# The last feed-forward chunk by token halves, and the last layer norm from row sums

## The reference

```python
def layer_norm(x, g, b):
    mu = mean(x); var = mean((x - mu)**2)
    return (x - mu) * rsqrt(var + 1e-5) * g + b
def swiglu(x, w_gate, w_up, w_down):
    return (silu(x @ w_gate) * (x @ w_up)) @ w_down
x = layer_norm(alpha*x + 0.5*swiglu(x, ffn1...), ln1)
x = layer_norm(alpha*x + hybrid_mixer(x), ln2)
x = layer_norm(alpha*x + memory_cross_attention(x, mem), ln3)
x = layer_norm(alpha*x + 0.5*swiglu(x, ffn2...), ln4)
```

## Time and profile before

| | us |
|---|---|
| median of 3 runs | 1303.44 |
| lowest and highest | 1303.38, 1303.83 |
| profiled execution, its own time | 1306.2 |
| its span, first to last instruction | 1304.4 |
| TensorE busy (matmuls) | 1268.3, 97% |
| VectorE busy | 715.5, 55% |
| ScalarE busy | 449.2, 34% |
| GpSimd busy | 90.4, 7% |
| mean granted TensorE clock | 0.992 |

### The profile page before, as it was taken

The page is one execution under the profiler, slowest core; times in us unless marked ns, Lnnn a source line. Parts: engine busy times, 40 slices in busy tenths (PEclk is TensorE's granted clock), DMA queues, the critical chain, the costliest instruction groups (busy, mean ns, idle before and its releaser), DMA issues.

```text
span 1304.4 us, 16284 instructions
## 1 busy us (share of the span) xinstructions
PE 1268.3 (97%) x6065; PEld 1050.1 (81%) x6065; DVE 715.5 (55%) x994; ACT 449.2 (34%) x699; POOL 90.4 (7%) x126
## 2 busy tenths in 40 slices
PE   7999999999998999999999999999999999999995
PEld 6888888888887887877778887888888888888884
DVE  4644444444475666565644557554664444444446
ACT  3322222222245654455533325342422222222221
POOL 2000000000032100001010030002300000000004
PEclk9999999999999999999999999999999999999998
DMA  7433333333327222222163205213343333333311
GB/s 228 144 96 96 96 96 96 96 96 96 96 66 211 81 82 71 59 56 59 49 209 98 96 33 177 82 49 97 97 129 96 96 96 96 96 96 96 96 48 65
DMA packets 163129, 128.03 MB, mean 98 GB/s; under 512 B 5120, under 2 KB 150544, under 8 KB 163088
## 3 DMA queue, kind: packets, MB, share of 16 engines
q1 hardware_dynamic: 159872, 116.44, 29.8%
q0 software_dynamic: 3008, 11.01, 2.4%
q10 hardware_dynamic: 208, 0.01, 0.0%
HBM read 123.25 MB, written 4.19 MB: 98 GB/s over the span
## 4 chain that ended last, share of the span: by engine, by line
PE 91%; DVE 3%; POOL 2%; DMA 1%; ACT 1%; issue 1%; SPq 0%; DVEq 0%; POOLq 0%; ACTq 0%
PE bank L601 19%; PE bank L603 19%; PE bank L602 19%; PE banks_scores L601 9%; PE banks_scores L603 9%; PE banks_scores L602 9%; PE bank L880 2%; PE bank L862 1%; DVE ring_lo L1406 1%; PE banks_scores L832 1%; PE banks_scores L831 1%; DVE stats L1438 1%; PE bank L619 1%; DMA raw<-in_ffn_w_gate 1%; DVE xT_lo L1406 1%
## 5 line engine op out<-in xcount | busy, mean ns | idle before, releaser
L1406 DVE TENSOR_TENSOR ring_lo<-raw,ring_hi 128x1024 fp32r<-128x1024 f32 x215 | 261.0, 1234 | 123.6 <-ACT ring_hi L1090 123.3
L601 PE MATMUL bank<-xT_hi,ring_hi 128*128 128x512 f32 (+1 forms) x728 | 280.6, 385 | 4.5 <-DVE ring_lo L1406 2.3
L1090 ACT ACTIVATE ring_hi<-raw 128x1024 fp32r<-128x1024 f32 x215 | 221.7, 1056 | 176.5 <-DMA raw<-in_ffn_w_up 89.4
L602 PE MATMUL bank<-xT_lo,ring_hi 128*128 128x512 f32 (+1 forms) x728 | 278.4, 382 | 0.0
L603 PE MATMUL bank<-xT_hi,ring_lo 128*128 128x512 f32 (+1 forms) x728 | 278.3, 382 | 0.0
L601 PEld LDWEIGHTS bank<-xT_hi,ring_hi 128*128 128x128 f32 x728 | 138.8, 191 | 31.0 <-issue 3.9
L603 PEld LDWEIGHTS bank<-xT_hi,ring_lo 128*128 128x128 f32 x728 | 138.7, 191 | 26.3
L602 PEld LDWEIGHTS bank<-xT_lo,ring_hi 128*128 128x128 f32 x728 | 138.9, 191 | 24.9
L601 PE MATMUL banks_scores<-xT_hi,ring_hi 128*128 128x512 f32 (+1 forms) x368 | 140.7, 382 | 0.0
L602 PE MATMUL banks_scores<-xT_lo,ring_hi 128*128 128x512 f32 (+1 forms) x368 | 140.3, 381 | 0.0
L603 PE MATMUL banks_scores<-xT_hi,ring_lo 128*128 128x512 f32 (+1 forms) x368 | 140.3, 381 | 0.0
(11 more groups left out here) (274 smaller groups left out, 1783.0 us busy)
## 6 DMA issues: line engine op xcount, KB each, us to landing
raw<-in_ffn_w_gate SPq DMA_DIRECT2D x44, 512.0 KB, 4.7
raw<-in_ffn_w_up SPq DMA_DIRECT2D x44, 512.0 KB, 4.4
raw<-in_ffn_w_down SPq DMA_DIRECT2D x44, 512.0 KB, 3.3
raw<-in_mix_w_in SPq DMA_DIRECT2D x34, 512.0 KB, 3.8
raw<-in_mem_w_k SPq DMA_DIRECT2D x8, 512.0 KB, 4.1
raw<-in_mix_w_out SPq DMA_DIRECT2D x8, 512.0 KB, 3.2
raw<-in_mem_w_v SPq DMA_DIRECT2D x8, 512.0 KB, 3.2
raw<-in_mem_w_q SPq DMA_DIRECT2D x8, 512.0 KB, 4.7
```

What stands on the lines that cost most here:

```text
L601: pe.matmul(dst, hi, mhi, start=start, stop=False)
L602: pe.matmul(dst, hi, mlo, start=False, stop=False)
L1090: nc.scalar.activation(dst, src, copy).then_inc(unit_hi, 1)
L1406: nc.vector.tensor_tensor(dst, src, hi.bitcast(F32), ALU.subtract).then_inc(done, 1)
```

## The change

In the second feed-forward layer the loop runs nine times. What is left (gate and up of chunks 20 and 21, the down pairs 9 and 10) is written out in a function `closing` on TensorE, ScalarE and VectorE. TensorE's order there is: gate and up of chunk 20; gate and up of chunk 21 for the first 256 tokens; pair 9 and then pair 10 for the tiles of blocks 0 and 1; gate and up of chunk 21 for the other 256 tokens; pair 9 for tiles 4 to 6, pair 10 for 4 and 5, pair 9 for tile 7, pair 10 for 6 and 7. Pairs 9 and 10 of a tile are accumulated in one PSUM bank, and VectorE adds a tile once for both. The hidden values of the pair 10 have buffers of their own (`end_hi`, `end_lo`), and those of chunk 21 are made in two token halves.

Blocks 0 and 1 are normed as before, with the gain on VectorE and the bias on GpSimd. For blocks 2 and 3 the two tile additions also give row sums; VectorE makes minus the mean of them and centres the block with the gains in one operation into `x_mid`; ScalarE squares the block less its mean with a running sum, and scales that and adds eps; GpSimd takes the power -0.5; VectorE finishes each block in two halves, and each half is stored by itself. A constant `eps` is filled at the start.

```diff
+                def closing(n, chunk, pair):          # TensorE
+                    def up_half(p):
+                        for m in range(2):
+                            ready(n + 4 + m)
+                            half_units(n + 4, 1, p, (m,), end_up)
+                    def down_part(j, units, hid, first, last):
+                        for m in range(2):
+                            mm = down_product(units, j, m, hid, first, last)
+                        return mm
+                    gate_up(0, n, chunk)
+                    pe.wait_ge(h_full, chunk)
+                    up_half(0)
+                    ready(n + 3)
+                    pe.wait_ge(h_lo_done, chunk)
+                    for p in range(2):
+                        for j in range(4 * p, 4 * p + 4):
+                            if p == 0:
+                                pe.wait_ge(sums, tile_sums(f, pair - 1, j + 5))
+                            else:
+                                pe.wait_ge(end_sums, j - 3)
+                            if j == 7:
+                                pe.wait_ge(end_lo_done, 3)
+                                for early in (4, 5):
+                                    down_part(early, n + 6, (end_hi, end_lo), False, True).then_inc(end_tiles, 1)
+                            down_part(j, n + 2, (h_hi, h_lo), True, False)
+                        ready(n + 7)
+                        pe.wait_ge(end_lo_done, 2 + p)
+                        for j in range(4) if p == 0 else (6, 7):
+                            down_part(j, n + 6, (end_hi, end_lo), False, True).then_inc(end_tiles, 1)
+                        if p == 0:
+                            up_half(1)
...
-                with pe.Fori(0, FF_PAIRS - 1) as i:
+                with pe.Fori(0, FF_PAIRS - 1 - f) as i:
...
+                def closing(n, chunk):                # ScalarE
...
+                    prep(n + 6)
+                    prep(n + 7)
+                    act.wait_ge(end_h, 1)
+                    high(end_hi[:, 0, :], hf[:, 0, :], end_hi_done)
+                    hidden_half(0)
+                    high_half(0)
+                    standardize(3, xb, 0)
+                    hidden_half(1)
+                    high_half(1)
+                    standardize(3, xb, 1)
+                    for b in range(2):
+                        act.wait_ge(end_mean, b + 1)
+                        nc.scalar.activation(squares[:, b, :], xb[:, 2 + b, :], ACT.Square, bias=neg_mean[:, 2 + b:3 + b],
+                                             accum_out=var[:, b:b + 1]).then_inc(end_var, 1)
+                        act.wait_ge(end_var, b + 1)
+                        nc.scalar.activation(var[:, b:b + 1], var[:, b:b + 1], ACT.Identity, scale=1.0 / D,
+                                             bias=eps[:, 0:1]).then_inc(eps_var, 1)
...
+                    hidden_half(0)                    # VectorE, behind the splits and chunk 20
+                    for b in range(2):
+                        end_tile(2 * b)
+                        end_tile(2 * b + 1)
+                        block_stats(3, x, b, end_sums, 2 * b + 2)
+                    gain(3, x, 0)
+                    hidden_half(1)
+                    gain(3, x, 1)
+                    end_tile(4)
+                    end_tile(5)
+                    centre(2)
+                    end_tile(6)
+                    end_tile(7)
+                    centre(3)
+                    finish(2)
+                    finish(3)
...
-            layer_norm(3, xb, 1)                      # GpSimd
+            for b in range(2):
+                inverse_deviation(3, b)
+            for b in range(2):
+                add_bias(3, xb, b)
+            for b in range(2):
+                pool.wait_ge(eps_var, b + 1)
+                nc.gpsimd.tensor_tensor(rstd[:, 2 + b:3 + b], var[:, b:b + 1], expo[:, :], ALU.pow).then_inc(end_rstd, 1)
```

## The result

| | before | after |
|---|---|---|
| median of the first comparison (4 runs each) | 1303.63 us | 1294.57 us, 0.9925 [0.9908, 0.9943] |
| median with the changed kernel run again (17 and 6 runs) | 1303.22 us | 1297.05 us, 0.9946 [0.9928, 0.9964] |
| all runs of either: lowest, mean, highest | 1301.3, 1304.1, 1307.5 (61 runs) | 1293.8, 1295.9, 1299.0 (10 runs) |
| profiled execution, its own time | 1306.2 | 1294.26 |
| span | 1304.4 | 1292.5 |

The change makes the kernel faster, by 9.06 us between the first medians. The forecast was 1296.5, range 1295.4 to 1298.5.

A forecast was written before the change was run, and what follows sets the result against it. TensorE, busy 97% of the span, was taken as the bound, followed by VectorE's tail. VectorE's end moves from 1301.94 to 1295.0, -6.9 including TensorE's +0.64; 1306.2 - 6.9 = 1299.3, less 2.8 for the median: 1296.5 us, range 1295.4 to 1298.5.

The forecast's parts named there:

- TensorE, +0.64, no gap: Closing matmuls: 96 of 256 columns replace 48 of 512, adding 0.64 us on the path; TensorE never stalls.
- The chain on VectorE, 5.22 plus 0.25: VectorE after the last matmul: tile 7, mean, centring, two finishings take 5.22 us, plus 0.25 waiting, ending at 1295.0.
- Power of block 3, a wait of 0.25: GpSimd's power for block 3's inverse deviation, partly held by VectorE's halves, ends at 1293.55 and delays finishing by 0.25 us.
- Gone: the queue of older blocks: VectorE at the last matmul: no older work ahead, 8 additions replace 16, tile 7 begins 0.42 us after that matmul's start.
- From the profiled execution to the median: Whole kernel: profiled 1306.2 less 6.9 gives 1299.3; the median lies 2.8 lower, so 1296.5 us.
- No table load: Rival, 10%: an activation table load at ScalarE's squares, or a held power, delays block 3's finishing: 1297.1 to 1298.3 us.
- no stall of TensorE: Rival, 4%: TensorE stalls in the closing part for a late second hidden half, and its clock falls: 1299.8 with 2 us late.
- halves at 0.12: Rival, 2%, the slower side: half products of chunk 21's gate and up cost as much as whole ones: 1306.8 us.
- tile 7 taken in time: Rival, 3%: GpSimd's bias additions or extra semaphore hops push VectorE's older work past 1289.55: 1297.5 to 1299.5 us.
- scalar-tensor-tensor of 128x1024 in 1.28 us: Rival, 1%: VectorE's centring and finishing on two SBUF tensors run at half speed, 3 x 1.2 us more: 1300.1 us.

The follow-up runs named there:

- finish_early: The changed kernel with the first half of finishing block 2 put on VectorE between the additions of tiles 6 and 7: 1296.18 us, 0.9948.
- sums_only: The kernel before, old TensorE order with 16 additions, given the new norm of blocks 2 and 3 from row sums and squares: expected -3.7 us, measured 1303.54 us, 0.9996.
- whole: The changed kernel with gate and up of chunk 21 in whole units of 512 columns, both ahead of the down pairs: 1297.05 us, 0.9946.

## Why the prediction was right or wrong

- **TensorE, +0.64, no gap.** Right: +0.68 (47.77 against 47.09), and 33.33 us without a pause. Each product and split on a hidden half took 0.41 or 0.42 us, as assumed, but one: the low part of the second half took 0.66, beside the bias addition of block 0, off the path.
- **The chain on VectorE, 5.22 plus 0.25.** Too long by 0.56: from the addition of tile 7 to the end it is 1290.03 - 1285.12 = 4.91. Of that 0.25 is the wait of the next point. The read of the sum ends with the addition, so that the next operation starts 0.73 us after it where I had 0.79; the mean takes 0.25 to the next start, not 0.27; successive operations overlap by 0.08 (1286.10 + 1.28 ends after 1287.30), and four halves take 2.73, not 2.88.
- **Power of block 3, a wait of 0.25.** Wrong: 0. It got through beside VectorE's halves in 0.70 us. The direction of my bound was right in finish_early, where it does become the limit by 0.44 us.
- **Gone: the queue of older blocks.** Right: tile 7 is taken 0.43 us after the start of the last matmul, where it had been 4.93. I priced the queue as VectorE's backlog alone; sums_only and whole show that the hold between VectorE and GpSimd can be a good part of it (2.1 and 1.3 us). Had I read the gain of 2.01 us beside the bias addition in the trace of before as a price (0.8 us each), sums_only's -3.7 would not have stood. In the forecast it did no harm, as the closing order keeps the two apart but for the 0.66 above.
- **From the profiled execution to the median.** This is the step that failed: "the terms are lengths of engine work that are in both", with "some tenths for another build's run". The terms were, but the rest of the kernel isn't a constant: before ranges over 6 us, its profiled execution was from its upper group (1306.2) and its first median from the lower. What I had put at some tenths was the difference of two draws of the first part, and only -7.39 of the -9.06 was the change. -7.39 from 1303.6 is 1296.2, inside the range: that the first four runs fell below it was the luck of their first parts (1236.5 to 1238.0). The six later runs have 1297.05 as median, inside it again, also by luck; all ten have 1295.9 as mean. A range honest about this would have been some 2 us wider on each side.
- **Rivals.** No table load, no stall of TensorE, halves at 0.12, tile 7 taken in time, scalar-tensor-tensor of 128x1024 in 1.28 us: none of the five came true. The Trainium skill's sentence on halved throughput ("Vector Engine (DVE) Microarchitecture Reference", Points that are easy to get wrong) does not hold for these operations, none of which has two SBUF sources and an accumulator output at once. The Trainium skill's rule on the shared ports ("SBUF — State Buffer", SBUF: two separate sides), an exclusive lock for the whole instruction, agrees with the runs for whole bias additions: 3.35 us beside one, 1.29 without.
- Open: which pause the clock falls behind in a given run.

## What to carry to other kernels

Before pricing a chain of element-wise work, look for what the neighbour engine does at the same time: here an operation on two SBUF tensors on VectorE and a bias addition on GpSimd didn't share time, one waited for the other (3.35 us for 1.29), and the order that keeps them apart was worth more (4.65 us) than the shorter norm without it (0.05). A 128x1 power got through between VectorE's halves with little loss (0.70 us for 0.57). Moving one of them without a pause for it only moves the wait. And compare the part that an edit touches, by a mark in the trace, before believing a difference of medians: where short pauses of TensorE leave its clock to luck, whole runs differ by several us for nothing.

## What the runs showed of the hardware that I had not expected

- VectorE's read of its accumulator is 0.08 us and lies wholly beside the addition (1285.73 + 0.08, the addition until 1285.81); ScalarE's is 0.18 to 0.19.
- A centring that meets a bias addition of GpSimd waits for its end and then needs 1.09 of its 1.28 us: what it has done while held is at most 0.2 us.
- Filling five pauses of TensorE with 74 idle transposes makes the kernel before faster by 3.5 us and its runs three times as even (1.6 us in eleven of its runs against 4.7).
